# A two-layer mixer and expert decoder on one core: every large on-chip tile moved to a multiple of 512 bytes

## The chip, the core and the metric

One core of a Trainium2 chip runs the whole program. TensorE (PE in the profile) multiplies matrices, VectorE (DVE) and ScalarE (ACT) work on elements, SyncE (SP) issues the loads, GpSimd (POOL) issues a few small transfers at the start. On-chip memory has 128 partitions. A tile is a stretch of the same bytes in each partition, so it has one start address, and this case is about these addresses. The metric is the device time of one execution in microseconds (us), as the median of the runs.

## The reference

The input is 256 tokens by 1024 channels, in float32. Two layers are applied:

```
for layer in range(2):
    x = x + hybrid_mixer(rms_norm(x, mix_norm_g[layer]), ...)    # one wide input projection, mLSTM + attention, gates, output projection
    h = rms_norm(x, ffn_norm_g[layer])
    if layer % 2 == 0:
        x = x + swiglu(h, gate, up, down)                        # dense, width 2816
    else:
        x = x + moe_swiglu(h, router_w, gates, ups, downs)       # top 2 of 8 experts, width 3584
swiglu(h, wg, wu, wd) = (silu(h @ wg) * (h @ wu)) @ wd
```

Each expert has three weight matrices of 1024 by 3584 values, 44 MB together, and all eight are read.

## The kernel before, in words

**Pieces.** All large weights go through one pipeline in pieces of 128 partitions by 1024 float32 values (4096 bytes in each partition). SP loads a piece into a slot of `raw`. In the expert part there are more slots: 12 pieces in `raw`, 7 in `more` and 2 in `toep`, a ring of 21 (the names `UNIT`, `PIECE`, `RING`). ScalarE writes the rounded value into `w_hi` (line 886), VectorE the rest into `w_lo` (line 1189), six pieces deep. TensorE then multiplies a piece in three products, high by high, high by low and low by high, so that float32 accuracy comes out of the fast `fp32r` format. `piece` does this for every weight in the program:

```
def piece(m, work, j=0):
    pe.wait_ge(s["w_lo_done"], piece_count(m, j))
    hi, lo = w_hi[:, m % PARTS, :], w_lo[:, m % PARTS, :]
    for o, (lh, ll), cols, first, swap in work:
        for n, (l, r) in enumerate(((lh, hi), (lh, lo), (ll, hi))):
            r = r[:, cols[0]:cols[1]]
            ins = mm(o, r if swap else l, l if swap else r, start=first and n == 0, stop=True,
                     skip_group_check=True)
    ins.then_inc(s["w_used"], 1)
```

The first operand of `mm` is the stationary one (128 columns, 512 bytes in each partition, loaded ahead of each matmul). The second is the moving one, 512 columns (2048 bytes) of the weights. A profile row `pA<-w_hi,hT_hi` has the moving operand first: `w_hi` moves and `hT_hi` is stationary. Only the first two chunks of a mixer (`swap`) have it the other way round.

**Stationary operands.** For the input projection, the output projection and every gate and up matrix they come from `hT_hi` and `hT_lo`, for the two branch projections from `g_hi` and `g_lo`. For the down matrices they come from `aT_hi` and `aT_lo` (dense) or `ex_hi` and `ex_lo` (experts), where the activations stand transposed. `spread` is stationary where an expert's result (`y_hi`, `y_lo`, moving) is put back to its tokens (line 814).

**Order.** Mixer 0, dense, mixer 1, router, then eight experts. An expert's 84 pieces go in seven rounds of 4 gate, 4 up and 4 down pieces. A piece is 6 matmuls there, and 12 in the dense part, where 256 tokens are done rather than 128. The orders are written out by hand, with semaphores; the changed kernel has the same instructions in the same order on each engine.

**Addresses.** Tiles are laid one behind the other in the order of their declaration, each start rounded up to 32 bytes. `raw` starts at byte 16512. The tiles declared with `mb` (mixer), `fb` (dense) and `eb` (experts) are three layouts over the same bytes, behind the lasting ones. Bytes past a multiple of 512 at which tiles start:

| tiles | before | changed |
|---|---|---|
| raw, w_hi, w_lo, x, hT_hi, hT_lo, g_hi, g_lo, cst, vec, toep | 128 | 0 |
| conv_in | 160 | 0 |
| qk, v, so, aqk, av, ga, gb (mixer) | 256 | 0 |
| aT_hi, aT_lo, sg, act (dense) | 160 | 0 |
| more, ex_hi, ex_lo, ex_sg, ex_act, pick, spread (experts) | 160 | 0 |
| y_hi, y_lo (experts) | 416 | 256 |

The 128-column slices taken of `hT`, `g`, `aT` and `ex` tiles start at multiples of 512 bytes within them, so the table holds for each slice too.

Of the kernel before, what the change touches and what calls it, by code (L numbers as in the profile page):

```python
# [12 lines left out]
P = 128  # L13
D = 1024
KT = D // P
S = 256
A = S // P
NL = 2
MH, MD = 4, 128
AH, AD = 8, 64  # L20
MW, AW = MH * MD, AH * AD
TAPS = 4
# [61 lines left out]
def program(nc, x_in, rel_bias, mix_norm_g, w_in, conv_w, conv_b, igate_b, fgate_b, mlstm_norm_g,  # L84
            q_norm_g, k_norm_g, w_branch_a, w_branch_b, w_out, ffn_norm_g, dense_gate, dense_up, dense_down,
            router_w, expert_gate, expert_up, expert_down, consts, bucket_hot, bucket_mask, bias_rows, out):
    with ExitStack() as ctx:
        def sb(name, shape, dt=F32):
            return ctx.enter_context(nc.sbuf_tensor(name, shape, dt))
# [2 lines left out]
            return ctx.enter_context(nc.semaphore(name))  # L92


        raw = sb("raw", [P, RAW, UNIT])
        w_hi = sb("w_hi", [P, PARTS, PIECE], F32R)
        w_lo = sb("w_lo", [P, PARTS, PIECE], F32R)
# [17 lines left out]
        wg_lo = sb("wg_lo", [P, KT, 8], F32R)  # L115


        mix = ExitStack()

        def mb(name, shape, dt=F32):  # L120
            return mix.enter_context(nc.sbuf_tensor(name, shape, dt))

        conv_in = mb("conv_in", [P, 2 * MH, TAPS - 1 + S])
        qk = mb("qk", [P, 2 * MH, S])
        v = mb("v", [P, A, MW])
        so = mb("so", [P, A, MW])
# [1 line left out]
        av = mb("av", [P, A, AW])  # L128
        ga = mb("ga", [P, A, D])
        gb = mb("gb", [P, A, D])  # L130
        mix.close()
        ffn = ExitStack()

# [1531 lines left out]
```

## Time and profile before

| | |
|---|---|
| median of 3 runs | 1676.85 us (1676.07 to 1677.97) |
| span of the profiled execution (its own time is not listed apart) | 1675.9 us |
| PE, DVE, ACT busy | 97%, 78%, 66% of the span |
| PE's share of the chain that ended last | 90% |
| loaded from memory | 452.69 MB, 271 GB/s over the span |

"Busy" is the share of the span in which an engine had a matmul or another operation under way. Since matmuls overlap, a busy PE does not say how fast they follow each other. For that the distance from one start to the next is read.

### The profile page before, as it was taken

How to read it: one execution, taken by the hardware profiler on the slowest of the kernel's cores; microseconds unless marked ns; L12 is line 12 of the kernel's file. 1: busy time of each engine (PE TensorE's matmuls, PEld its weight loads, DVE VectorE, ACT ScalarE, POOL GpSimd, SP SyncE). 2: the span in 40 equal slices, each digit the busy share in tenths (PEclk: the TensorE clock that was granted, in tenths of full speed). 3: DMA queues.
4: the chain of work that ended last, by engine and by line, in shares of the span. 5: the costliest groups of instructions: out<-in, count | busy, mean ns of one | idle time of the engine just before them, and what ended most of it. 6: DMA issues, size and time to landing. Idle time of an engine off the chain costs nothing.

```text
span 1675.9 us, 23876 instructions
## 1 busy us (share of the span) xinstructions
PE 1622.1 (97%) x7759; PEld 1337.6 (80%) x7759; DVE 1300.9 (78%) x1582; ACT 1104.4 (66%) x1373; POOL 7.5 (0%) x17
## 2 busy tenths in 40 slices
PE   6999989999899997999999999999999999999998
PEld 5877878888787776888888888888888888888886
DVE  4865655445586565888988988988988988988987
ACT  5547444344565744777777777777777777777775
POOL 1000000000000000000000000000000000000000
PEclk9999999999999997999999999999999999999999
DMA  9533545555344455999998998998998998998991
GB/s 305 190 126 126 176 140 187 187 176 190 126 155 136 142 172 188 315 387 313 352 388 316 352 387 315 354 388 314 349 384 320 348 389 319 347 386 319 357 380 57
DMA packets 204624, 454.91 MB, mean 271 GB/s; under 512 B 13752, under 2 KB 15936, under 8 KB 204528
## 3 DMA queue, kind: packets, MB, share of 16 engines
q1 hardware_dynamic: 202880, 452.57, 75.8%
q0 software_dynamic: 592, 1.20, 0.3%
q8 instruction: 39, 0.64, 0.2%
q14 instruction: 57, 0.47, 0.1%
q10 hardware_dynamic: 1056, 0.03, 0.0%
HBM read 452.69 MB, written 1.06 MB: 271 GB/s over the span
## 4 chain that ended last, share of the span: by engine, by line
PE 90%; DVE 5%; ACT 3%; issue 1%; DMA 0%; SPq 0%; ACTq 0%; DVEq 0%
PE pA L446 73%; PE pB L446 8%; PE pB L465 3%; PE pB L791 2%; DVE w_lo L1189 1%; PE pB L814 1%; DVE hT_lo L1556 1%; ACT w_hi L886 1%; PE pA L492 1%; ACT hT_hi L1117 0%; PE pA L465 0%; DMA aqk<-mlstm_norm_g_dram 0%; PE pB L613 0%; DVE ex_lo L1589 0%; DVE small L1335 0%
## 5 line engine op out<-in xcount | busy, mean ns | idle before, releaser
L1189 DVE TENSOR_TENSOR w_lo<-raw,w_hi 128x1024 fp32r<-128x1024 f32 x570 | 668.1, 1221 | 129.5 <-ACT w_hi L886 122.7
L886 ACT ACTIVATE w_hi<-raw 128x1024 fp32r<-128x1024 f32 x570 | 577.8, 1058 | 117.4 <-PE pA L446 77.9
L446 PE MATMUL pA<-w_hi,hT_hi 128*128 128x512 f32 (+1 forms) x1376 | 544.0, 395 | 0.6 <-DVE hT_lo L1210 0.6
L446 PE MATMUL pA<-w_hi,hT_lo 128*128 128x512 f32 (+1 forms) x1376 | 535.4, 389 | 0.0
L446 PE MATMUL pA<-w_lo,hT_hi 128*128 128x512 f32 (+1 forms) x1376 | 534.4, 388 | 0.0
L446 PEld LDWEIGHTS pA<-w_hi,hT_lo 128*128 128x128 f32 x1376 | 259.5, 189 | 54.5
L446 PEld LDWEIGHTS pA<-w_hi,hT_hi 128*128 128x128 f32 x1376 | 259.9, 189 | 52.2 <-DVE w_lo L1189 1.1
L446 PEld LDWEIGHTS pA<-w_lo,hT_hi 128*128 128x128 f32 x1376 | 260.0, 189 | 50.6 <-issue 0.2
L1189 DVE TENSOR_TENSOR w_lo<-more,w_hi 128x1024 fp32r<-128x1024 f32 x224 | 263.0, 1221 | 23.3 <-ACT w_hi L886 22.8
L886 ACT ACTIVATE w_hi<-more 128x1024 fp32r<-128x1024 f32 x224 | 230.2, 1060 | 43.1 <-PE pA L446 42.6
L446 PE MATMUL pA<-w_hi,ex_hi 128*128 128x512 f32 x448 | 178.3, 398 | 2.8 <-DVE ex_lo L1589 2.8
L446 PE MATMUL pA<-w_hi,ex_lo 128*128 128x512 f32 x448 | 177.3, 396 | 0.0
L446 PE MATMUL pA<-w_lo,ex_hi 128*128 128x512 f32 x448 | 177.0, 395 | 0.0
L446 PEld LDWEIGHTS pA<-w_hi,ex_hi 128*128 128x128 f32 x448 | 84.1, 188 | 25.1 <-DVE w_lo L1189 5.0
L1142 ACT ACTIVATE ex_hi<-pB 128x512 fp32r<-128x512 f32 x56 | 33.8, 604 | 103.0 <-PE pB L465 103.0
L446 PEld LDWEIGHTS pA<-w_hi,ex_lo 128*128 128x128 f32 x448 | 84.1, 188 | 20.2
L446 PEld LDWEIGHTS pA<-w_lo,ex_hi 128*128 128x128 f32 x448 | 84.2, 188 | 19.8
L1189 DVE TENSOR_TENSOR w_lo<-toep,w_hi 128x1024 fp32r<-128x1024 f32 x64 | 76.9, 1222 | 13.7 <-ACT w_hi L886 13.7
L1589 DVE TENSOR_TENSOR ex_lo<-pB,ex_hi 128x512 fp32r<-128x512 f32 x56 | 38.6, 690 | 38.2 <-ACT ex_hi L1142 38.2
L886 ACT ACTIVATE w_hi<-toep 128x1024 fp32r<-128x1024 f32 x64 | 65.4, 1069 | 2.7 <-PE pA L446 2.7
L1138 ACT ACTIVATE ex_sg<-pA 128x512 f32<-128x512 f32 x56 | 33.5, 598 | 23.2 <-PE pA L446 23.1
L1585 DVE TENSOR_TENSOR ex_act<-pA,ex_sg 128x512 f32<-128x512 f32 x56 | 38.5, 687 | 2.8 <-PE pA L446 2.8
(282 smaller groups left out, 1441.7 us busy)
## 6 DMA issues: line engine op xcount, KB each, us to landing
raw<-expert_w_gate_dram SPq DMA_DIRECT2D x160, 512.0 KB, 5.9
raw<-expert_w_up_dram SPq DMA_DIRECT2D x128, 512.0 KB, 5.7
raw<-expert_w_down_dram SPq DMA_DIRECT2D x96, 512.0 KB, 5.6
raw<-w_in_dram SPq DMA_DIRECT2D x44, 1024.0 KB, 5.1
more<-expert_w_down_dram SPq DMA_DIRECT2D x88, 512.0 KB, 5.5
more<-expert_w_up_dram SPq DMA_DIRECT2D x80, 512.0 KB, 5.7
more<-expert_w_gate_dram SPq DMA_DIRECT2D x56, 512.0 KB, 6.0
toep<-expert_w_down_dram SPq DMA_DIRECT2D x40, 512.0 KB, 5.1
```

Of the source, the lines that this page charges most:

```text
L446: ins = mm(o, r if swap else l, l if swap else r, start=first and n == 0, stop=True, skip_group_check=True)
L465: return mm(o, src, ident, is_transpose=True, start=first, stop=True, skip_group_check=True)
L492: ins = mm(B2[0:8, 0:S], l[:, k, :], r[:, k, :], start=(k == 0 and n == 0), stop=True, skip_group_check=True)
L791: ins = mm(o[:, i, :], src[:, a, P * k:P * (k + 1)], pick[:, a, :], start=(i == 0 and n == 0), stop=True, skip_group_check=True)
L814: ins = mm(o, spread[:, a, :], src[:, 512 * half:512 * (half + 1)], start=(n == 0), stop=(n == 1))
L886: f(w_hi[:, m % PARTS, :], raw_slot(m), ACT.Copy).then_inc(s["w_hi_done"], 1)
L1138: f(ex_sg[:], B0, ACT.Silu).then_inc(s["silu_done"], 1)
L1142: f(ex_hi[:, c % 2], bank_as(B4, 4, P), ACT.Copy).then_inc(s["aT_hi_done"], 1)
L1189: tt(w_lo[:, m % PARTS, :], raw_slot(m), w_hi[:, m % PARTS, :].bitcast(F32), ALU.subtract).then_inc(s["w_lo_done"], 1)
L1556: ins = stt(hT_lo[:, k, 0:P], pB[:, 1 + b, P * i:P * (i + 1)], col(R_FFNG + KT + k), hT_hi[:, k, 0:P].bitcast(F32), ALU.mult, ALU.subtract)
L1585: tt(ex_act[:], B1, ex_sg[:], ALU.mult).then_inc(s["act_done"], 1)
L1589: tt(ex_lo[:, c % 2], bank_as(B4, 4, P), ex_hi[:, c % 2].bitcast(F32), ALU.subtract).then_inc(s["aT_lo_done"], 1)
```

## The change

Two tiles that nothing reads or writes are declared as padding (384 bytes ahead of `raw`, 480 bytes ahead of the mixer, dense and expert layouts), and `conv_in`, whose length is not a multiple of 512 bytes, goes from the first to the last place of the mixer's layout.

```
+        sb("to_line", [P, 96])
         raw = sb("raw", [P, RAW, UNIT])
...
         wg_lo = sb("wg_lo", [P, KT, 8], F32R)
+        sb("to_line2", [P, 120])
         mix = ExitStack()
...
-        conv_in = mb("conv_in", [P, 2 * MH, TAPS - 1 + S])
         qk = mb("qk", [P, 2 * MH, S])
         v = mb("v", [P, A, MW])
...
         gb = mb("gb", [P, A, D])
+        conv_in = mb("conv_in", [P, 2 * MH, TAPS - 1 + S])
         mix.close()
```

No instruction, wait or transfer is added, removed or moved. Only addresses change.

## Rows read from the trace of the kernel before

**Rows 1.** The profile page: span, busy time, chain that ended last.

```profile
span 1675.9 us, 23876 instructions
PE 1622.1 (97%) x7759; PEld 1337.6 (80%) x7759; DVE 1300.9 (78%) x1582; ACT 1104.4 (66%) x1373; POOL 7.5 (0%) x17
PE 90%; DVE 5%; ACT 3%; issue 1%; DMA 0%; SPq 0%; ACTq 0%; DVEq 0%
```

**Rows 2.** Chain in order of time: start us, us, what.

```profile
194.44 10.90 PE pB L446 x48
336.20 16.36 PE pA L446 x72
352.56 11.20 PE pB L446 x48
861.27 16.52 PE pA L446 x72
```

**Rows 3.** Timeline of PE in one expert: start us, us, operation.

```profile
829.94 0.39 PE L446 MATMUL pA<-w_hi,hT_hi 128*128 128x512 f32 x1
...
835.15 0.40 PE L446 MATMUL pA<-w_hi,hT_lo 128*128 128x512 f32 x1
835.39 0.39 PE L446 MATMUL pA<-w_hi,ex_hi 128*128 128x512 f32 x1
...
840.98 0.39 PE L446 MATMUL pA<-w_hi,hT_hi 128*128 128x512 f32 x1
```

**Rows 4.** Line 446 and tile g_hi: count, duration ns min/median/max.

```profile
L446 PE MATMUL pA<-w_hi,hT_hi x1376: 278/389/796, 47.5 to 1655.8; 128*128 128x512 f32 x193, 128*128 128x256 f32 x4
L446 PE MATMUL pA<-w_hi,ex_hi x448: 392/395/502, 692.9 to 1667.4; 128*128 128x512 f32 x150
L446 PE MATMUL pB<-w_hi,aT_hi x88: 392/395/476, 284.7 to 426.4; 128*128 128x512 f32 x88
L446 PE MATMUL pA<-hT_hi,w_hi x128: 278/283/682, 20.2 to 463.1; 128*128 128x256 f32 x128
L446 PE MATMUL pB<-w_hi,g_hi x32: 389/389/389, 194.3 to 615.1; 128*128 128x512 f32 x32
```

**Rows 5.** Tile spread: its matmuls, durations as above.

```profile
L814 PE MATMUL pB<-y_hi,spread x30: 391/396/481, 799.1 to 1670.4; 128*128 128x512 f32 x30
L814 PE MATMUL pB<-y_lo,spread x30: 387/392/397, 799.3 to 1670.7; 128*128 128x512 f32 x30
```

**Rows 6.** Waits of the whole run: us in total, times, longest.

```profile
ACT w_hi L886 <- PE pA L446: 123.2, 210, 2.5
SPq L359 <- DVE w_lo L1189: 640.2, 628, 28.6
```

**Rows 7.** Windows: busy us (instructions), PEclk, DMA share, GB/s.

```profile
640.00:668.00 28.00, 18.95 (x96) 16.26 (x96) 18.04 (x59) 10.31 (x25) 0.00 (x0) 0.72 0.37 141
718.84:735.80 16.96, 16.96 (x77) 13.89 (x77) 15.10 (x14) 13.14 (x14) 0.00 (x0) 1.00 1.03 390
```

**Rows 8.** The page's groups: count | busy us, mean ns | idle before.

```profile
L1189 DVE TENSOR_TENSOR w_lo<-raw,w_hi 128x1024 fp32r<-128x1024 f32 x570 | 668.1, 1221 | 129.5 <-ACT w_hi L886 122.7
L886 ACT ACTIVATE w_hi<-raw 128x1024 fp32r<-128x1024 f32 x570 | 577.8, 1058 | 117.4 <-PE pA L446 77.9
L1189 DVE TENSOR_TENSOR w_lo<-more,w_hi 128x1024 fp32r<-128x1024 f32 x224 | 263.0, 1221 | 23.3 <-ACT w_hi L886 22.8
L886 ACT ACTIVATE w_hi<-more 128x1024 fp32r<-128x1024 f32 x224 | 230.2, 1060 | 43.1 <-PE pA L446 42.6
```

**Rows 9.** Lines 465 and 1286: count, duration ns min/median/max.

```profile
L465 PE MATMUL pB<-cst,ex_act x224: 270/272/273, 683.6 to 1659.6; 128*128 128x128 f32 x112
L465 PE MATMUL pB<-cst,aqk x81: 270/273/447, 10.3 to 584.1; 128*128 128x128 f32 x81
L1286 DVE SCALAR_TENSOR_TENSOR qk<-conv_in,vec,qk x48: 483/485/488, 53.2 to 488.9; 128x256 f32<-128x256 f32 x48
```

**Rows 10.** Chain: the gather of two experts; the start of the program.

```profile
4.63 5.50 DMA aqk<-mlstm_norm_g_dram
660.51 7.09 PE pB L791 x32
772.48 3.52 PE pB L791 x32
```

More of the change, by code:

```diff
@@ L92, in sem @@
             return ctx.enter_context(nc.semaphore(name))
+        sb("to_line", [P, 96])
         raw = sb("raw", [P, RAW, UNIT])
@@ L115, in program @@
         wg_lo = sb("wg_lo", [P, KT, 8], F32R)
+        sb("to_line2", [P, 120])
         mix = ExitStack()
@@ L121, in mb @@
             return mix.enter_context(nc.sbuf_tensor(name, shape, dt))
-        conv_in = mb("conv_in", [P, 2 * MH, TAPS - 1 + S])
         qk = mb("qk", [P, 2 * MH, S])
@@ L130, in program @@
         gb = mb("gb", [P, A, D])
+        conv_in = mb("conv_in", [P, 2 * MH, TAPS - 1 + S])
         mix.close()
```

## The prediction

> **What bounds the kernel now.** I read the page first. PE is busy for 97% of the span and makes up 90% of the chain that ended last; DMA has 0% of it [rows 1]. The waits say who is ahead of whom. ScalarE's next piece waits for TensorE to free a slot of `w_hi`, 123.2 us in all, and SP's loads wait 640.2 us for slots that VectorE has not yet given back [rows 6]. Loads, ScalarE and VectorE are all ahead, and TensorE sets the pace. So an address can only pay if it changes the distance between matmuls, and the chain in order of time is where that distance is read.
>
> **The distance depends on the stationary tile.** In the dense part six pieces with `hT` stationary take 16.36 us for 72 matmuls, 227.2 ns each. The four down pieces behind them, with `aT` stationary, take 11.20 us for 48, which is 233.3 ns each [rows 2]. In an expert, from 829.94 to 835.15 us there are 23 steps with `hT` stationary, 5.21 / 23 = 226.5 ns. From 835.39 to 840.98 there are 24 steps with `ex`, 5.59 / 24 = 232.9 ns [rows 3]. The durations say the same: 389 ns at the median with `hT` or `g_hi` stationary, 395 ns with `ex_hi` or `aT_hi` [rows 4].
>
> What sets the 395 ns matmuls apart? It is not the moving operand, which is `w_hi` or `w_lo` in all. It is not the output tile either: `pB` takes both 389 ns (with `g_hi`) and 395 ns (with `aT_hi`) [rows 4]. The 48 matmuls of a branch projection go to `pB` in 10.90 us, 227.1 ns each [rows 2]. It is not one stage, since both kinds alternate in one expert. What is left, of what I can see, is where the stationary tile lies. `hT` and `g` start 128 bytes past a multiple of 512, which is a multiple of 64. `aT` and `ex` start 160 bytes past one, which is a multiple of 32 alone. `spread`, at 160 too, gives 396 and 392 ns [rows 5]. The change takes every one of them to 0.
>
> **The sum, part by part.**
>
> *Down matrices of the experts.* There are three groups of 448 matmuls with `ex` stationary (one of them stands in [rows 4]), 1344, in 56 runs of 24. A run has one more long distance, the one that leads into it: from 835.15 to 840.98 there are 25 distances in 5.83 us, where 25 at 226.5 ns would take 5.66. That is 0.17 us a run, and 56 runs give 9.5 us. Check on the chain: 72 matmuls of an expert, 24 of them down, take 16.52 us against 16.36 us for 72 without down [rows 2], 0.16 us.
>
> *Down matrix of the dense part.* Three groups of 88, 264 matmuls at 233.3 - 227.2 = 6.1 ns, 1.6 us.
>
> *`spread`.* Some 32 matmuls at 7 ns and 32 at 3 ns over 389 [rows 5], 0.3 us. The sum so far is 11.4 us. I take 11.0, since at the handover between experts the chain leaves TensorE for a few us and a saving there can be lost.
>
> *`hT`, `g`, `w_hi`, `w_lo` from 128 to 0.* These carry the other three quarters of the matmuls, and no large tile of the trace starts at 0, so this price is not shown. From below: `y_hi` and `y_lo` move from 416 past a multiple of 512, not a multiple of 64, and their matmuls are no slower than those with `ex` (396 and 392 against 395) [rows 4, 5]. The start of the moving operand seems to cost nothing, so 128 to 0 would give nothing there. From above: the one step that the trace shows is 6.4 ns. If the stationary rows lost as much again between 128 and 0, the about 4900 others (three groups of 1376 to `pA`, the 384 swapped ones, three of 64 to `pB`, six of 32 with `g`) would give 4900 x 6.4 ns = 31 us. The same 31 us is the bound for a loss. I take nothing, because the nearest row is that from 160 to 128, and what that removes is a start off a multiple of 64, which 128 does not have.
>
> *Transposes.* With `ex_act` (at 160) stationary 272 ns, with `aqk` (at 256) 273 ns [rows 9]. No gain.
>
> *VectorE and ScalarE.* Line 1189 takes 1221 ns out of `raw` (128) and out of `more` (160), line 886 takes 1058 and 1060 ns [rows 8]. The convolution's sources start at all kinds of offsets, and its 48 instructions take 483 to 488 ns [rows 9]. Nothing, and TensorE would cover it.
>
> *Loads.* They land at other addresses. SP waits for slots and not the other way round [rows 6], so quicker loads would be hidden. Only the first loads of the program are on the chain, 5.50 us until the small vectors have landed [rows 10]. They are short, and a tenth of it would be 0.5 us. I count nothing.
>
> *Does the cover hold?* A round of 12 pieces would take 16.8 us in place of 16.96. VectorE has 15.10 us of work in it, so it is at 90%. The loads need 6.3 MB in 16.8 us, 374 GB/s, and 390 GB/s were moved over one such round [rows 7]. If one of the two did bind, the saving of 0.17 us a round would shrink, at worst to nothing.
>
> The total is 11.0 us. The span of 1675.9 becomes 1664.9, and the median, which stands 0.95 above the span, becomes 1665.9.
>
> **A rule that speaks against it.** The Trainium skill, page "TensorE: Matmul & The Clock Gate", section "Step-by-step: what each phase is for", says that TensorE reads SBUF through two independent ports and that loading the next weights takes no read bandwidth from the matmul that runs. "SBUF — State Buffer", section "Door 1: The DMA port swizzle", knows lines of 16 bytes only, and 128, 160 and 0 are all multiples of 16. By these two the sum would be nothing, 1676.85 us, and the 6 ns would have some other cause. The trace does not bear out the first in full: the tile of the load alone goes with 389 or 395 ns.
>
> **The rivals.**
>
> *The address is not the cause (no change).* `aT`, `ex` and `spread` differ from `hT` and `g` in one more thing: they lie higher, in the last quarter of the memory, and they stay there. If the region made the 6 ns, the time would stay at 1676.9, give or take 1. Against it: nothing in the rows shows a dependence on height, and `hT` and `g` lie far apart and agree. It can't be excluded. It is also what the two pages give. 14%.
>
> *128 to 0 pays too (much faster).* Then up to 31 us more, and any part of it: 1635 to 1663 us, about 1635 if the same step comes once more. For it: the matmuls with 512 moving columns last 389 ns and the swapped ones with 256 last 283 [rows 4], so 256 columns cost 106 ns and 512 cost 212. The distance of 226.5 ns is 14 ns over that, so something is left to be won. Against it: nothing ties these 14 ns to an address. 13%.
>
> *A multiple of 512 is itself a bad place (slower).* No row has a stationary or moving tile there. If the stationary load and the moving rows, both now at 0, met in the same part of the memory and delayed each matmul, all 6500 would pay. The gain of 11 us is used up from 11 / 4900 = 2.2 ns for each of the others, and the loss is over 0.2% from 2.9 ns. At the 6.4 ns seen it would be 1676.9 - 11 + 31 = 1697. Against it: `hT` and `w_hi` stand in the same place modulo 512 already (both 128), and these are the 389 ns rows. 7%.
>
> *The clock.* From 640 to 668 us the granted clock is 0.72 of 2.4 GHz, behind the router's gaps, and a gather there takes 7.09 us against 3.52 us later [rows 7, 10]. If another stretch falls to 1.2 GHz as the gaps shift, that costs up to 3.6 us, or gives it back. This widens the range and is no case of its own.
>
> **How the numbers follow.** Forecast 66%: 1665.9, its own range 1663.5 to 1668.5 (the sum from 9.5 to 11.4, and the clock). No change 14%, much faster 13%, slower 7%. To hold 8 in 10 the range goes up to the no-change case at 1677.5, and down to 1661, into the near part of the much faster case. A measurement of this kernel can tell about 0.2%, 3.4 us, from no change. Faster by more than that: 66 + 13 = 79%, less 1 for a forecast that is mostly hidden. Within it: 15. Slower: 7.
>
> **What would show it.** Right: the median of the `ex_hi`, `aT_hi` and `spread` matmuls falls from 395 to 389 ns, 48 dense down matmuls take 10.9 us on the chain, 72 of an expert 16.3 to 16.4 us, and the `hT` rows stay at 389. Busy times of VectorE and ScalarE stay. Wrong: `ex_hi` stays at 395 (region), the `hT` and `g_hi` rows move from 389 down or up, or the matmuls quicken while PE begins to wait for `w_lo` and the span stays.

## The result, and the profile after

The changed kernel takes 1669.57 us at the median of four runs (1667.10 to 1670.07), the kernel before 1677.41 us beside it (1676.07 to 1679.49). The ratio is 0.9949, 95% interval 0.9936 to 0.9963, a gain of about 8 us. The forecast was 1665.9 us, which is 0.9935 of the 1676.85 us shown with the kernel before.

The page of the changed kernel, to be held against [rows 1]. The engines have the same work, and PE still makes up 90% of the chain. Only its busy time moved, by 8 us. All line numbers are 2 higher than before.

```profile
span 1668.0 us, 23876 instructions
PE 1614.1 (97%) x7759; PEld 1338.5 (80%) x7759; DVE 1300.9 (78%) x1582; ACT 1104.3 (66%) x1373; POOL 7.5 (0%) x17
PE 90%; DVE 5%; ACT 3%; issue 2%; DMA 0%; SPq 0%; ACTq 0%; DVEq 0%
```

The matmul rows of the changed kernel (count, duration ns min/median/max) answer to [rows 4, 5]. `ex` and `aT` went from 395 ns to 389, `hT` stayed at 389, and `spread` went from 396 to 391.

```profile
L448 PE MATMUL pA<-w_hi,hT_hi x1376: 278/389/793, 47.5 to 1648.4; 128*128 128x512 f32 x193, 128*128 128x256 f32 x4
L448 PE MATMUL pA<-w_hi,ex_hi x448: 387/389/500, 692.8 to 1659.7; 128*128 128x512 f32 x150
L448 PE MATMUL pB<-w_hi,aT_hi x88: 389/389/476, 284.8 to 424.8; 128*128 128x512 f32 x88
L816 PE MATMUL pB<-y_hi,spread x30: 389/391/481, 798.0 to 1662.7; 128*128 128x512 f32 x30
```

The chain of the changed kernel in order of time (start us, us, what) answers to [rows 2].

```profile
194.64 10.90 PE pB L448 x48
...
335.69 16.36 PE pA L448 x72
352.06 10.88 PE pB L448 x48
...
859.70 16.36 PE pA L448 x72
...
911.59 11.17 PE pA L448 x48
...
1036.17 11.16 PE pA L448 x48
```

A round of dense down matmuls takes 10.88 us in place of 11.20. An expert's round takes 16.36 in place of 16.52. The first run of matmuls behind a handover starts at 911.59 us and that behind the next at 1036.17, a period of 124.58 us. In the kernel before these points stand at 913.46 and 1038.99, a period of 125.53:

```profile
913.46 11.30 PE pA L446 x48
...
1038.99 11.31 PE pA L446 x48
```

So an expert gained 0.95 us, where seven runs of 24 down matmuls at 0.17 us each would give 1.19. About one run of the seven stands where the chain leaves TensorE between two experts, and its saving is mostly lost.

Where did the rest of the 11 us go? VectorE and ScalarE are unchanged: 1220 and 1058 ns against 1221 and 1058 [rows 8]. ScalarE waits a little less for a free slot, 117.1 us against 123.2 [rows 6]. Groups of the page of the changed kernel, then one line of its waits:

```profile
L1191 DVE TENSOR_TENSOR w_lo<-raw,w_hi 128x1024 fp32r<-128x1024 f32 x570 | 668.0, 1220 | 128.5 <-ACT w_hi L888 121.7
L888 ACT ACTIVATE w_hi<-raw 128x1024 fp32r<-128x1024 f32 x570 | 577.5, 1058 | 111.9 <-PE pA L448 74.4
```

```profile
ACT w_hi L888 <- PE pA L448: 117.1, 210, 2.5
```

What did move is the granted clock. Windows of the changed kernel, in the second mixer and behind the router (start:end, length, busy us and count of PE, PEld, DVE, ACT, POOL, then PEclk, DMA share, GB/s):

```profile
535.00:547.00 12.00, 9.40 (x46) 7.28 (x46) 10.37 (x15) 7.50 (x8) 0.00 (x0) 0.86 0.66 233
640.00:668.00 28.00, 18.78 (x91) 15.33 (x90) 16.75 (x58) 9.93 (x24) 0.00 (x0) 0.66 0.31 122
```

The same window at 535 us in the kernel before has the clock at 1.00; that behind the router had 0.72 [rows 7].

```profile
535.00:547.00 12.00, 9.41 (x54) 7.33 (x53) 11.09 (x13) 9.45 (x12) 0.00 (x0) 1.00 0.65 208
```

A granted clock of 0.86 or 0.66 over a window means that TensorE stood at 1.2 GHz for part of it and at 2.4 GHz for the rest. From the same matmul to the same matmul, the second mixer's middle took 96.24 us (493.90 to 590.14) against 95.41 before (496.03 to 591.44), and the router's 36.06 us (624.35 to 660.41) against 34.87 (625.64 to 660.51). That is 2.0 us given back. The bookkeeping of these two executions is thus: up to the second mixer's middle -2.1, most of it the dense part's down matrix, those two stretches +2.0, and the experts -7.8, which makes the 7.9 us between the spans.

### The profile page after: what moved, and what is told of

It reads as the page before. It is cut to its first block, busy times and chain, and to the rows that moved or that the text cites. A ratio compares the mean times of both kernels' runs of the same rounds, so it can differ in the third digit from the quotient of the medians.

```text
span 1668.0 us, 23876 instructions
## 1 busy us (share of the span) xinstructions
PE 1614.1 (97%) x7759; PEld 1338.5 (80%) x7759; DVE 1300.9 (78%) x1582; ACT 1104.3 (66%) x1373; POOL 7.5 (0%) x17
## 4 chain that ended last, share of the span: by engine, by line
PE 90%; DVE 5%; ACT 3%; issue 2%; DMA 0%; SPq 0%; ACTq 0%; DVEq 0%
PE pA L448 73%; PE pB L448 7%; PE pB L467 3%; PE pB L793 2%; DVE w_lo L1191 1%; PE pB L816 1%; DVE hT_lo L1558 1%; PE pA L494 1%; ACT w_hi L888 1%; ACT hT_hi L1119 0%; PE pA L467 0%; DMA aqk<-mlstm_norm_g_dram 0%; PE pB L615 0%; DVE ex_lo L1591 0%; PE pB L641 0%
## 5 line engine op out<-in xcount | busy, mean ns | idle before, releaser
L1191 DVE TENSOR_TENSOR w_lo<-raw,w_hi 128x1024 fp32r<-128x1024 f32 x570 | 668.0, 1220 | 128.5 <-ACT w_hi L888 121.7
L888 ACT ACTIVATE w_hi<-raw 128x1024 fp32r<-128x1024 f32 x570 | 577.5, 1058 | 111.9 <-PE pA L448 74.4
L1191 DVE TENSOR_TENSOR w_lo<-more,w_hi 128x1024 fp32r<-128x1024 f32 x224 | 262.9, 1220 | 23.2 <-ACT w_hi L888 23.0
L448 PEld LDWEIGHTS pA<-w_hi,ex_lo 128*128 128x128 f32 x448 | 84.1, 188 | 17.7
L1191 DVE TENSOR_TENSOR w_lo<-toep,w_hi 128x1024 fp32r<-128x1024 f32 x64 | 76.8, 1221 | 13.7 <-ACT w_hi L888 13.7
```

Of the source, the lines that this page charges most:

```text
L888: f(w_hi[:, m % PARTS, :], raw_slot(m), ACT.Copy).then_inc(s["w_hi_done"], 1)
L1191: tt(w_lo[:, m % PARTS, :], raw_slot(m), w_hi[:, m % PARTS, :].bitcast(F32), ALU.subtract).then_inc(s["w_lo_done"], 1)
```

## The experiments

Each kernel is the changed one with the edit shown, run beside the kernel before, and all of them compute everything. "At 32" means a start 32 bytes past a multiple of 512. In the lines of the pads, `[P, 8]` is 32 bytes and `[P, 120]` is 480.

### The same change again, the second pad alone, the first pad alone, everything at 32

The first of these runs is the changed kernel itself, on another chip (1668 to 1670 us were expected).

> The changed kernel once more, as the mark for the three others beside it: 0.995 of the kernel before, some 1668 to 1670 us, with 389 ns for matmuls with ex_hi stationary. If the granted clock falls in other places than in its first profile (there it fell for one more 3.4 us stretch at 539.5 us and one more at 645 us), the span should move by about 1 us for each.

The second leaves out the first pad. Every large tile is then at 128, with `y` at 384.

```
-        sb("to_line", [P, 96])
```

> Only the pad ahead of the layouts and the move of conv_in: all tiles, raw, w_hi, hT, aT and ex alike, start 128 bytes past a multiple of 512. Theory (a stationary row costs 6.4 ns more if it starts off a multiple of 64 bytes): ex_hi and aT_hi rows at 389 ns, time as the changed kernel, 0.995. Rival (it is the multiple of 512 that counts): ex_hi stays at 395 ns, time as before, 1.000.

The third leaves out the second pad: `w`, `hT` and `g` at 0, `aT`, `ex` and `spread` at 32.

```
-        sb("to_line2", [P, 120])
```

> Only the pad ahead of raw and the move of conv_in: raw, w_hi, w_lo, hT, g at 0, and the layouts (aT, ex, more, mixer) at 32 past a multiple of 512. Theory: ex_hi, aT_hi and spread rows stay at 395 ns, hT rows at 389, time as before, 1.000 (0.999 to 1.001). Rival (the lower tiles at 0 give part of the gain, through loads or the moving operand): up to 0.995.

The fourth makes the first pad 32 bytes longer, so that every large tile is at 32.

```
-        sb("to_line", [P, 96])
+        sb("to_line", [P, 104])
```

> All tiles at 32 past a multiple of 512. Theory: every group of line 446's matmuls goes to 395 ns (289 for the swapped ones with 256 moving columns); the 4900 matmuls that were at 389 before lose 6.4 ns each, 31 us: about 1708 us, 1.019. Rival (the region of memory, not the start, made ex and aT slower): hT and g rows stay at 389 ns, time as before, 1.000.

| kernel | moving at | `hT`, `g` at | `aT`, `ex` at | median us | ratio to before [95%] |
|---|---|---|---|---|---|
| change again | 0 | 0 | 0 | 1667.1 | 0.9937 [0.9919, 0.9954] |
| second pad only | 128 | 128 | 128 | 1668.85 | 0.9942 [0.9927, 0.9958] |
| first pad only | 0 | 0 | 32 | 1677.5 | 0.9996 [0.9986, 1.0006] |
| all at 32 | 32 | 32 | 32 | 1668.03 | 0.9941 [0.9925, 0.9957] |

The matmuls of the kernel with the first pad only:

```profile
L447 PE MATMUL pA<-w_hi,hT_hi x1376: 278/389/799, 47.5 to 1654.6; 128*128 128x512 f32 x193, 128*128 128x256 f32 x4
L447 PE MATMUL pA<-w_hi,ex_hi x448: 392/395/504, 691.7 to 1666.2; 128*128 128x512 f32 x150
```

And those of the kernel with all at 32:

```profile
L448 PE MATMUL pA<-w_hi,hT_hi x1376: 278/389/793, 47.6 to 1651.2; 128*128 128x512 f32 x193, 128*128 128x256 f32 x4
L448 PE MATMUL pA<-w_hi,ex_hi x448: 389/389/504, 695.5 to 1662.5; 128*128 128x512 f32 x150
```

The second pad alone gives the whole gain. The first alone gives nothing: its interval, 0.9986 to 1.0006, holds the time before. The region of memory is out as a cause, since `ex` keeps its place high in the memory in all four and has 389 ns in three of them (change again and second pad only have it too). My reading of the cause falls too: with `hT`, `w_hi` and `ex` all at 32, no multiple of 64, nothing is slower, where I expected 1.019. What the 395 ns rows share is that their stationary tile stands 32 bytes off the moving one. The new theory was therefore the distance between the two starts, and the next runs made distances on purpose.

### The distance made on purpose

Here only the moving tiles `w_hi` and `w_lo` are at 32, the rest at 0.

```
+        sb("off", [P, 8])
         w_hi = ...
         w_lo = ...
+        sb("on", [P, 120])
```

> The changed kernel with w_hi and w_lo alone at 32 past a multiple of 512; they are the moving operand of all but 384 matmuls, and written by ScalarE and VectorE. Theory (only the stationary start counts): the rows with hT_hi and ex_hi stationary stay at 389 ns; only the 384 swapped ones, where w is stationary, go from 283 to 289 ns: 2.5 us, 0.9965 of before. Rival (the moving start counts as well): all rows go to 395 ns, some 42 us more, 1.02.

Here only the stationary `hT_hi` and `hT_lo` are at 32, by the same two pads around them.

> The changed kernel with hT_hi and hT_lo alone at 32 past a multiple of 512. Theory: their about 4300 matmuls go to 395 ns, ex_hi stays at 389: 4300 x 6.4 = 28 us more than the changed kernel, 1.011 to 1.012 of before. Rival (the moving and the stationary start must differ from each other by a multiple of something, or it is the region): no change, 0.995. The swapped matmuls, with hT moving, should stay at 283 ns.

The ratios are 1.012 [1.0095, 1.0145] at 1698.75 us, and 1.0063 [1.0042, 1.0084] at 1687.47 us. Moving tiles at 32 first, then `hT` at 32:

```profile
L450 PE MATMUL pA<-w_hi,hT_hi x1376: 278/396/793, 47.0 to 1678.0; 128*128 128x512 f32 x193, 128*128 128x256 f32 x4
L450 PE MATMUL pA<-w_hi,ex_hi x448: 392/396/497, 701.0 to 1689.6; 128*128 128x512 f32 x150
```

```profile
L450 PE MATMUL pA<-w_hi,hT_hi x1376: 277/396/795, 47.0 to 1663.3; 128*128 128x512 f32 x193, 128*128 128x256 f32 x4
L450 PE MATMUL pA<-w_hi,ex_hi x448: 387/390/499, 692.9 to 1674.6; 128*128 128x512 f32 x150
L450 PE MATMUL pA<-hT_hi,w_hi x128: 277/280/682, 20.2 to 460.5; 128*128 128x256 f32 x128
```

The distance is the cause of the 395 ns, made here from either side: with the moving tiles off, every 512-column row of line 450 rises, and with `hT` off, only its own. For the first kernel my theory, that only the stationary start counts, forecast 0.9965, and it failed. By the ratios the two cost some 31 and 21 us over the change, where 42 (the rival's price) and 28 were on record. A part of what is missing is known. The 256-column matmuls with the roles swapped take 280 ns here against 283 [rows 4], so they pay nothing, 2.5 us of the 42. The handovers hide some more: from handover to handover the two kernels take 127.38 us (924.63 to 1052.01) and 126.53 us (914.96 to 1041.49) against the change's 124.58, so eight experts cost 22.4 and 15.6 us, where 504 and 336 matmuls an expert at 6.6 ns would make 26.6 and 17.7. The last 4 to 5 us of each lie ahead of the experts, where the granted clock moves too, and I can't split them.

### What else the change did

The loads' target `raw` alone at 32, everything else as in the change:

```
-        sb("to_line", [P, 96])
+        sb("to_line", [P, 104])
         raw = sb("raw", [P, RAW, UNIT])
+        sb("on", [P, 120])
```

> The changed kernel with raw alone at 32 past a multiple of 512; the loads write it, ScalarE and VectorE read it, no matmul does. Theory: nothing, 0.995. Rival (part of the gain came through the loads): slower than the changed kernel, 0.996 to 0.999, with landing times over 5.7 us for the gate pieces.

And `conv_in` put back to the first place, so that the mixer's tiles behind it are at 96:

```
+        conv_in = mb("conv_in", [P, 2 * MH, TAPS - 1 + S])
         qk = mb("qk", [P, 2 * MH, S])
...
-        conv_in = mb("conv_in", [P, 2 * MH, TAPS - 1 + S])
```

> Both pads, but conv_in stays first in the mixer's layout, so that the mixer's tiles lie at 96 past a multiple of 512; w, hT, g, aT, ex at 0. By all theories that stand, only fp32r matmuls pay for addresses, and these use no mixer tile: time as the changed kernel, 0.994 of before. Rival (the mixer's tiles give a share): 0.995 to 0.998.

They give 0.9936 [0.9911, 0.9961] at 1666.04 us, and 0.9937 [0.9912, 0.9961] at 1669.08 us. Both have the whole gain. Where the loads land and where the mixer's tiles stand is worth nothing that these runs can tell, which is about 0.25% by their intervals.

### Other distances

In these kernels the stationary tiles are slices of longer tiles, begun some elements late, for example:

```
-        ex_hi = eb("ex_hi", [P, 2, 4, P], F32R)
+        ex_hi = eb("ex_hi", [P, 8 * P + P], F32R)[:, 4:4 + 8 * P].rearrange(...)
```

First `aT` and `ex` 16 bytes off:

> The changed kernel with aT and ex tiles 16 bytes past a multiple of 512 (a view into a longer tile). If a stationary row is fetched in stretches of 64 bytes and any start off them costs the same: 395 ns, 1.000 of before. Rival (what counts is a start off a multiple of 16 bytes, or the cost grows with the distance from 64): 389 ns or a value between, 0.995 to 0.998.

Then `hT` at 16, `ex` at 48, `aT` at 8 and `g` at 4:

> w at 0; hT 16, ex 48, aT 8 and g 4 bytes off it. New theory after the runs with all tiles at 32 (389 ns) and w or hT alone at 32 (395): what costs is a distance of 32 bytes, modulo 64, between the start of the moving and of the stationary operand; 16 bytes cost nothing at the median. If only 32 costs: all rows 389 ns, about 0.995. If the cost rises to its most at 32 and 48 is as 16: the same. If any distance over 16 costs: ex at 395, hT at 389, 1.000. Rival (8 and 4 bytes cost, as they are off a multiple of 16): aT and g rows at 395 ns, some 2 us.

Then `ex` at 96, `aT` at 64 and `g` at 160, with `hT` at 0:

> w and hT at 0; ex 96, aT 64 and g 160 bytes off. Theory (distance modulo 64): ex (32 modulo 64) at 395 ns, aT (0) at 389, g (32) at 395; ex costs 9 us: about 0.999 to 1.000. Rival (modulo 128 or more): aT at 64 changes too, or ex at 96 stays at 389.

The first gives 0.996 [0.9946, 0.9975] at 1670.05 us, the second 1.0086 [1.0063, 1.0109] at 1691.56 us, the third 1.0015 [1.0004, 1.0027] at 1680.42 us. The matmuls of the three, in this order:

```profile
L448 PE MATMUL pA<-w_hi,ex_hi x448: 388/390/500, 687.6 to 1657.1; 128*128 128x512 f32 x150
L448 PE MATMUL pB<-w_hi,aT_hi x88: 388/390/475, 281.2 to 421.4; 128*128 128x512 f32 x88
```

```profile
L448 PE MATMUL pA<-w_hi,hT_hi x1376: 277/394/796, 47.2 to 1667.2; 128*128 128x512 f32 x193, 128*128 128x256 f32 x4
L448 PE MATMUL pA<-w_hi,ex_hi x448: 390/396/499, 693.9 to 1678.9; 128*128 128x512 f32 x150
L448 PE MATMUL pB<-w_hi,aT_hi x88: 391/392/482, 282.5 to 424.3; 128*128 128x512 f32 x88
L448 PE MATMUL pA<-w_hi,g_hi x32: 388/392/399, 181.9 to 604.4; 128*128 128x512 f32 x32
```

```profile
L448 PE MATMUL pA<-w_hi,ex_hi x448: 391/397/500, 696.4 to 1672.5; 128*128 128x512 f32 x150
L448 PE MATMUL pB<-w_hi,aT_hi x88: 393/394/478, 285.3 to 427.1; 128*128 128x512 f32 x88
L448 PE MATMUL pA<-w_hi,g_hi x32: 394/394/394, 183.5 to 607.4; 128*128 128x512 f32 x32
```

These medians have to be held against the chain, which has the distances from start to start. The first two lines are of the second kernel (a branch projection with `g` at 4, then a dense down round with `aT` at 8), the next two of the third (`aT` at 64, then an expert's round with `ex` at 96):

```profile
193.21 11.17 PE pB L448 x48
...
282.71 11.08 PE pB L448 x48
```

```profile
285.42 11.20 PE pB L448 x48
...
722.39 16.56 PE pA L448 x72
```

Against 10.90, 10.88 and 16.36 us in the changed kernel, a matmul pays 6 ns at a distance of 4 bytes, 4 ns at 8, 7 ns at 64 and some 8 ns at 96 (0.20 us over 24 `ex` matmuls). For 4 bytes the median duration (392 ns) had shown only half of the price. The rows with 48 and 160 bytes stand 7 and 5 ns over 389. So every distance but 0 that was tried costs something, 16 bytes only at times. That 64 costs rules out "the same place modulo 64", on which the third kernel was built. The second kernel was off too: the most that I had on record for it was 1.000, with the `hT` rows at 389 ns.

At 16 bytes the price is paid in some rounds in full and in others not at all. With `ex` at 16, the rounds of 72 cost nothing (16.36 to 16.38 us), but the first round behind each handover costs 11.31 us as before the change, where the change has 11.17:

```profile
906.89 11.31 PE pA L448 x48
...
946.30 16.38 PE pA L448 x72
```

The median of 390 ns hides this: about a third of the `ex` matmuls follow each other in 233.3 ns and the others in 226.7, always a whole stretch between two interruptions at one of the two, at the same places in nearly every expert. With `hT` at 16, three of four dense rounds are free and one is not, and the expert rounds (48 `hT` at 16 and 24 `ex` at 48) take 16.71 and 16.80 us, where the full price for the `ex` alone would make 16.52 [rows 2]:

```profile
300.26 16.32 PE pA L448 x72
...
334.13 16.79 PE pA L448 x72
...
846.49 16.80 PE pA L448 x72
...
863.73 16.71 PE pA L448 x72
```

What decides between the two at 16 bytes is open.

### Whose distance: the load's, or the matmul's

Only `hT_lo` is at 32, so one stationary tile in three is off.

```
         hT_hi = sb("hT_hi", [P, KT, S], F32R)
+        sb("off", [P, 8])
         hT_lo = sb("hT_lo", [P, KT, S], F32R)
+        sb("on", [P, 120])
```

> The changed kernel with hT_lo alone at 32. The three products of a piece have hT_hi, hT_hi, hT_lo stationary. If the load of the next stationary operand beside the running moving one is what costs: only the distance from the second product's start to the third's is long (hT_lo is loaded then), a third of all, 1440 x 6.4 = 9 us, 0.999 to 1.000. If a matmul's own pair of operands costs: only the distance behind the third. If both, two thirds, 18 us: 1.005.

The ratio is 1.0058 [1.004, 1.0077], as much as with both `hT` tiles off. It is that of five executions with a median of 1686.28 us. A sixth took 6358.81 us, which no other execution of any kernel here came near, and its cause is not known; with it the median is 1687.27. The kernel's matmuls, and four of them in the timeline (start us, us):

```profile
L450 PE MATMUL pA<-w_hi,hT_hi x1376: 278/395/796, 47.1 to 1664.7; 128*128 128x512 f32 x193, 128*128 128x256 f32 x4
L450 PE MATMUL pA<-w_lo,hT_hi x1376: 277/400/628, 47.4 to 1664.9; 128*128 128x512 f32 x193, 128*128 128x256 f32 x4
L450 PE MATMUL pA<-w_hi,hT_lo x1376: 278/389/628, 47.6 to 1665.2; 128*128 128x512 f32 x193, 128*128 128x256 f32 x4
```

```profile
850.12 0.40 PE L450 MATMUL pA<-w_hi,hT_hi 128*128 128x512 f32 x1
850.36 0.40 PE L450 MATMUL pA<-w_lo,hT_hi 128*128 128x512 f32 x1
850.60 0.39 PE L450 MATMUL pA<-w_hi,hT_lo 128*128 128x512 f32 x1
850.83 0.40 PE L450 MATMUL pA<-w_hi,hT_hi 128*128 128x512 f32 x1
```

Three matmuls take 0.71 us, where 3 x 226.7 ns would be 0.68. On the chain a dense round of 72 with `hT` takes 16.80 us, as with both tiles off (16.79 and 16.80), and in the changed kernel 16.34 to 16.36. The time alone would have passed for two thirds of the price as well (1.005 was on record for that); the round doesn't.

The steps say where it is paid. Averaged over all of the trace outside pauses and stretches at a low clock, the distance to the next start is 232 ns behind `w_hi,hT_hi`, 238 behind `w_lo,hT_hi` and 229 behind `w_hi,hT_lo`, where the changed kernel has 227 to 228 for each. So some 11 ns of the 16 or so are paid while `w_lo` runs and `hT_lo`, the tile that is off, is loaded, and most of the rest one matmul earlier. The matmul that itself uses the off tile pays 1 ns or so. This speaks for the load beside a running matmul and against a matmul's own pair of operands. But it is more than the 6.4 ns that one load was to cost, and a load of `hT_hi` ahead of it pays too. As they were on record both rules fall.

## Why the prediction was right, and where it wasn't

**TensorE sets the pace, so only the distance of matmuls counts: right.** DVE and ACT kept their times, and the span followed PE.

**395 ns becomes 389 for `ex` and `aT`: right, in size too.** The dense down rounds went from 11.20 to 10.88 us, the experts' rounds from 16.52 to 16.36 us.

**The sum of 11.0 us: too high by 3 us in this comparison.** The 1669.57 us stand inside the range, but a microsecond over the forecast's own range (1663.5 to 1668.5). The term of the experts' down matrices was 9.5 us and measured 7.8, since seven runs an expert gave 0.95 us and not 1.19. I had named the handover but taken off only 0.4 us for it. The clock took back 2.0 us in the profiled execution, within the up to 3.6 us that the prediction left for it. On the other chip the ratio was 0.9937, some 10.6 us. There, the executions at a mean granted clock of 0.991 took 1675.92 to 1676.64 us before and 1665.12 and 1666.46 us changed, which is 10.6 us again. So at equal clock the sum was nearly right.

**Where the stationary tile lies, and whether that is a multiple of 64: wrong.** It is the distance between the stationary and the moving tile. The forecast held because the change sets both to the same place, and that was luck: by the rule as I had it, the kernel with all tiles at 32 should have lost 31 us against the kernel before, and it gained as much as the change. In [rows 4] the 389 ns rows all had both at 128, and the 395 ns rows had 160 against 128. I wrote "It is not the moving operand, which is `w_hi` or `w_lo` in all", and counted its start as costing nothing. A quantity that is constant in all rows can still be one half of a difference. `spread` was no support either. It stands 256 bytes from `y` before and after, and its row is not steady: the changed kernel has 391 ns for `y_hi` in one execution and 395 in the other. These matmuls come four at a time between others, and what they follow and precede may count as much as their own distance. I leave that row open.

**Nothing for `hT`, `g` and `w` from 128 to 0: right.** With both at 128 (second pad only) the ratio is 0.9942, with both at 0 it is 0.9937.

**Nothing for VectorE, ScalarE, the transposes and the loads: right**, by the kernels with `raw` at 32 and with the mixer's tiles at 96.

**The rivals.** The region is excluded. A second step from 128 to 0 does not show (0.9942 against 0.9937). The slower case, a bad place at a multiple of 512, did not occur, and the evidence that I set against it (`hT` and `w_hi` in the same place modulo 512) was in fact the reason for the 389 ns.

**The page's rule.** The Trainium skill, "TensorE: Matmul & The Clock Gate", section "Step-by-step: what each phase is for", has TensorE read through two independent ports. For these fp32r matmuls the runs don't bear that out in full: the same instructions follow each other in 226.7 or 233.3 ns, depending on where the two operands start relative to each other.

**Open.** Why the distance costs, why a single off tile in three costs the full price, what decides at 16 bytes between the full price and none, and what distances of 128 or 256 between `w` and `hT` do (not tried) was not settled.

## What to carry to other kernels

Start the stationary and the moving tiles of fp32r matmuls at the same remainder. A multiple of 512 bytes does it, and so did 128 and 32 for all; one pad of the right length ahead of the second region was worth the whole gain here, and the other pad and the reordering nothing. Before looking for such a gain, compare the median durations of like matmuls by tile: two levels some 6 ns apart are the sign. Then take the distance from start to start on the chain, since a median hides a price that only a third of the matmuls pay. What TensorE gains where the chain has left it is lost, as at the handovers here. And when two groups differ in one operand's address, list the addresses of both operands before naming the cause.

## What was not expected of the hardware

A 512-column fp32r matmul costs 226.7 ns from start to start with both operands at the same remainder and 233.3 ns with 32 bytes between them, 2.9% more. Over the kernel that is some 31 us, from a shift of 32 bytes. At 16 bytes a stretch of matmuls runs at one of these two distances or at the other, and at none between.

The swapped matmuls with 256 moving columns do not pay it. They took 280 ns at a distance of 32 (the kernel with `hT` off) against 283 at none.

The same program on the same chip varies with the clock that it is granted. Six executions of the changed kernel on the second chip have spans from 1663.2 us at a mean granted clock of 0.992 to 1671.1 us at 0.987. The profile of the one with 1670.7 us shows stretches at a lower clock in the first mixer (0.83) and behind the router (0.81).

```profile
140.00:150.00 10.00, 9.01 (x37) 6.50 (x36) 3.29 (x7) 7.51 (x14) 0.00 (x0) 0.83 0.24 86
...
640.00:668.00 28.00, 18.37 (x100) 15.14 (x99) 18.20 (x56) 13.33 (x27) 0.00 (x0) 0.81 0.50 197
```

That spread of 8 us is nearly as large as the gain, so a single pair of runs of this kernel can't be trusted to show it.
